# A transformer layer on one core: one modulation unit on TensorE and rounded activations first, with two value slots of the first heads inside the gate chunks

## The reference

```python
mod = silu(c) @ w_ada + b_ada                    # six vectors: sh1 sc1 gt1 sh2 sc2 gt2
h = rmsnorm(x, g_pre_mix) * (1 + sc1) + sh1
proj = h @ w_in                                  # gla q,k,v,r | rank-16 gate | moba q,k,v | gate_a, gate_b
y_a = (rmsnorm(gla_chunked(q, k, v, log_a)) * silu(gr)) @ w_gla_out      # 4 heads, dk 128, dv 256
y_b = moba_attention(mq, mk, mv) @ w_moba_out                            # 8 heads of 128, causal
y = (sigmoid(gate_a) * y_a + sigmoid(gate_b) * y_b) @ w_o
x = x + gt1 * rmsnorm(y, g_post_mix)
h = rmsnorm(x, g_pre_ffn) * (1 + sc2) + sh2
y = (gelu(conv3(h @ w_up)[g]) * conv3(h @ w_up)[u]) @ w_down
x = x + gt2 * rmsnorm(y, g_post_ffn)
```

## Time and profile before

| | |
|---|---|
| median of three runs | 1459.37 us (1457.54 to 1459.59) |
| profiled execution | 1459.07 us |
| its span | 1457.3 us |
| TensorE busy | 1422.6 us |
| VectorE busy | 1086.8 us |
| ScalarE busy | 760.2 us |
| DMA | 367.06 MB, mean 252 GB/s |
| granted TensorE clock | 0.999 |

### The profile page before, as it was taken

How to read it: one execution, slowest core, us unless ns; L and a number is a source line. 1 busy time by engine, 2 the same in 40 slices (tenths; PEclk the granted TensorE clock), 3 DMA queues, 4 the chain that set the end, 5 groups by cost and what they waited for, 6 DMA issues and landing times.

```text
span 1457.3 us, 19864 instructions
## 1 busy us (share of the span) xinstructions
PE 1422.6 (98%) x7296; PEld 1210.8 (83%) x7296; DVE 1086.8 (75%) x1161; ACT 760.2 (52%) x913; POOL 84.5 (6%) x165
## 2 busy tenths in 40 slices
PE   4999999999999999999999999999999999999998
PEld 3788788888888888878888888888888888888886
DVE  6899779898989878855787787777777766545545
ACT  5567763564545465443855545454555455443443
POOL 2000001111111100000000000000000000000000
PEclk9999999999999999999999999999999999999999
DMA  9999979998989777848477777677675555555653
GB/s 352 380 366 375 364 245 365 287 314 278 321 262 314 254 251 251 290 169 316 141 250 243 233 243 222 210 234 242 223 237 186 189 183 192 197 190 189 201 188 129
DMA packets 240569, 367.06 MB, mean 252 GB/s; under 512 B 12015, under 2 KB 178673, under 8 KB 239746
## 3 DMA queue, kind: packets, MB, share of 16 engines
q1 hardware_dynamic: 220576, 294.69, 60.9%
q0 software_dynamic: 18848, 69.23, 13.3%
q10 hardware_dynamic: 1090, 2.40, 0.4%
HBM read 364.18 MB, written 2.10 MB: 251 GB/s over the span
## 4 chain that ended last, share of the span: by engine, by line
PE 89%; ACT 3%; DMA 3%; DVE 3%; issue 1%; ACTq 0%; SPq 0%; DVEq 0%
PE ps L1465 88%; DMA raw<-in_w_in 2%; ACT hi L515 1%; DMA raw<-in_w_moba_out 1%; DMA rows<-in_b_conv 1%; ACT ps L556 0%; DVE lo L908 0%; DMA ada<-in_w_ada 0%; PE ps L1534 0%; DVE acc_a L937 0%; DVE yt L1285 0%; ACT h L561 0%; DVE x L1288 0%; ACT xn L543 0%; PE ps L1727 0%
## 5 line engine op out<-in xcount | busy, mean ns | idle before, releaser
L1465 PE MATMUL ps<-hT,hi 128*128 128x512 f32 x1936 | 466.2, 393 | 2.3 <-ACT ps L556 0.8
L1465 PEld LDWEIGHTS ps<-hT,hi 128*128 128x128 f32 x1936 | 355.8, 188 | 74.2 <-ACT ps L556 1.3
L515 ACT ACTIVATE hi<-raw 128x2048 fp32r<-128x2048 f32 (+1 forms) x123 | 222.3, 1808 | 241.5 <-DMA raw<-in_w_in 157.4
L908 DVE TENSOR_TENSOR lo<-raw,hi 128x2048 fp32r<-128x2048 f32 (+1 forms) x123 | 264.4, 2151 | 78.9 <-ACT hi L515 78.6
L1465 PEld LDWEIGHTS ps<-hT,lo 128*128 128x128 f32 x1920 | 246.1, 191 | 9.8 <-DVE lo L908 0.5
L1465 PE MATMUL ps<-hT,lo 128*128 128x256 f32 x1920 | 249.2, 283 | 0.1
L1413 DVE TENSOR_TENSOR lo<-raw,hi 128x2048 fp32r<-128x2048 f32 x88 | 199.0, 2290 | 33.3 <-ACT hi L851 32.9
L1465 PE MATMUL ps<-hi,hT 128*128 128x512 f32 x768 | 187.1, 394 | 3.2 <-DVE hT L962 2.1
L1465 PE MATMUL ps<-hi,asp 128*128 128x512 f32 x704 | 175.8, 389 | 0.0
L1465 PEld LDWEIGHTS ps<-hi,hT 128*128 128x128 f32 x768 | 141.9, 188 | 36.2 <-issue 4.4
L851 ACT ACTIVATE hi<-raw 128x2048 fp32r<-128x2048 f32 x88 | 165.7, 1906 | 9.4 <-DMA raw<-in_w_up 8.1
(11 more groups left out here) (262 smaller groups left out, 1317.3 us busy)
## 6 DMA issues: line engine op xcount, KB each, us to landing
raw<-in_w_up SPq DMA_DIRECT2D x176, 512.0 KB, 4.4
raw<-in_w_in SPq DMA_DIRECT2D x146, 512.0 KB, 6.0
ada<-in_w_ada POOLq DMA_DIRECT2D x128, 512.0 KB, 5.3
raw<-in_w_down SPq DMA_DIRECT2D x88, 512.0 KB, 4.1
adar<-in_w_ada SPq DMA_DIRECT2D x64, 384.0 KB, 8.2
raw<-in_w_o SPq DMA_DIRECT2D x32, 512.0 KB, 4.8
adar<-in_w_ada SPq DMA_DIRECT2D x16, 512.0 KB, 9.3
raw<-in_w_gla_out SPq DMA_DIRECT2D x16, 512.0 KB, 4.8
```

Source lines behind the costliest of these rows:

```text
L515: act.activation(hi[:, w % 4, 0:n], raw[:, w % 4, 0:n], ACT.Copy).then_inc(hi_done, 1)
L908: dve.tensor_tensor(lo[:, w % 4, 0:n], raw[:, w % 4, 0:n], hi[:, w % 4, 0:n].bitcast(F32), ALU.subtract).then_inc(lo_done, 1)
L1465: return pe.matmul(out_, lhsT, rhs, start=start, stop=stop, skip_group_check=open_sum)
```

## The change

Three things change together. **One unit on TensorE:** unit 12 of chunk 0 no longer goes through VectorE; six small products of its weights with the column `scol[:, 12]` open the sums in PSUM, and the sum of the other units is added to them. Three `spare` products go. The transposes of x start once its first 512 columns are scaled. **Rounded activations first:** for the first half of slot 0 VectorE writes the rounded h straight from x, TensorE multiplies it at once, and the products with the remainder of h come last. **Two value slots:** the first value slot (step 6) of heads 0 and 1 is moved to the middle of chunks 1 and 2, behind s = 3. ScalarE saves its sums in `vpart`, and copies them back to PSUM in step 5 of the head; step 6 has no slot any more, and decay products 0 to 3 move one step ahead in these heads. `vpart` takes the place of two `ada` buffers until the copies are done, so POOL uses three buffers instead of five up to unit 40.

```diff
+    GATE, VALUE, LOW = "gate", "value", "low"
+    EARLY = 2
...
+            if s_ == 3 and 1 <= q_ <= EARLY:
+                GATE_SLOTS.append((VALUE, q_, q_ - 1))
...
+    def head_steps(I):
+        return [n for n in range(HEAD_N) if n != 6 or I >= EARLY]
...
+    def gram_step(I, p):
+        return p + 3 if I >= EARLY or p > 3 else p + 2
...
+    PE_UNIT = 12
...
-    WIDE_FROM, WIDE_TO, THREE_TO = 8, 68, 86
+    THREE_FROM, WIDE_FROM, WIDE_TO, THREE_TO = 8, 40, 68, 86
...
+                if u == THREE_FROM:
+                    pool.wait_ge(tri_done, 1)
                 if u == WIDE_FROM:
-                    pool.wait_ge(tri_done, 1)
+                    pool.wait_ge(value_seed, EARLY)
...
-            for tt in range(TT):
-                act.activation(xn[:, tt, :], xn[:, tt, :], ACT.Copy, scale=stat[:, 2 + tt:3 + tt]).then_inc(xn_ready, 1)
+            for cs in (slice(0, 512), slice(512, D)):
+                for tt in range(TT):
+                    act.activation(xn[:, tt, cs], xn[:, tt, cs], ACT.Copy, scale=stat[:, 2 + tt:3 + tt]).then_inc(xn_ready, 1)
...
+                if kind == VALUE:
+                    act.wait_ge(used, w + 1)
+                    act.activation(vpart[:, s, :, :], ps[:, 6:8, :], ACT.Copy).then_inc(value_copy, 1)
...
-                    split_hi(w + 3)
+                    if streamed:
+                        split_hi(w + 3)
+                    if n == 5 and I < EARLY:
+                        b = 2 * group_pair(I, 3)
+                        act.wait_ge(evac, 5 * I + 3)
+                        act.activation(ps[:, b:b + 2, :], vpart[:, I, :, :], ACT.Copy).then_inc(value_seed, 1)
...
             for k in (0, 1):
-                ins = dve.tensor_scalar(h32[:, k, :], xT[:, k, TOK:], mods[:, M_SC1, k:k + 1], mods[:, M_SH1, k:k + 1], ALU.mult, ALU.add)
-            link(ins)
-            link(dve.tensor_copy(hT[:, 0:2, 0:TOK], h32[:, 0:2, :]))
-            dve.tensor_tensor(hT[:, 0:2, TOK:], h32[:, 0:2, :], hT[:, 0:2, 0:TOK].bitcast(F32), ALU.subtract).then_inc(h_ready, 1)
+                ins = dve.tensor_scalar(hT[:, k, 0:TOK], xT[:, k, TOK:], mods[:, M_SC1, k:k + 1], mods[:, M_SH1, k:k + 1], ALU.mult, ALU.add)
+            ins.then_inc(first_h, 1)
...
+                if b == 4:
+                    pe.wait_ge(cols_read, 2)
+                    pe.wait_ge(unit_in[PE_UNIT % 8], 32)
+                    for half in range(2):
+                        ins = unit_sums(half, unit_view(PE_UNIT), scol[:, PE_UNIT:PE_UNIT + 1], True)
+                    ins.then_inc(unit_used, 1)
...
-            for u in (KT - 3, KT - 2, KT - 1):
-                pe.wait_ge(unit_done, u)
-                spare(1)
...
+                if kind == VALUE:
+                    pe.wait_ge(sum_read, 2 * (K0[q + 1] - K0[1]))
+                    pe.wait_ge(hi_done, w + 1)
+                    tokens_still(w % 4, hT, 0, 6, True, True, w + 1).then_inc(used, 1)
+                    continue
...
+                    if n == 7 and I < EARLY:
+                        pe.wait_ge(value_seed, I + 1)
```

More of the change, by code:

```diff
@@ L64, in gate_at @@
     def gate_at(w):
-        q, s = divmod(w if w < W_LOW else w - 1, 8)
-        return q, s
+        return GATE_SLOTS[w][1:] if w < W_HEAD and GATE_SLOTS[w][0] == GATE else (None, None)
     def gate_stays(q, s):
@@ L349, in load_head @@
                 elif 6 <= n <= 9:
[L350 to L351 removed]
+                    load_values(w, I, 4 * (n - 6))
                 else:
@@ L570, in _ @@
             act.activation(hi[:, 0, 0:1024], raw[:, 0, 0:1024], ACT.Copy).then_inc(half_hi, 1)
-            act.wait_ge(arr[0], fills(0))
-            act.activation(hi[:, 0, 1024:slot_elements(0)], raw[:, 0, 1024:slot_elements(0)], ACT.Copy).then_inc(hi_done, 1)
+            act.wait_ge(first_ready, 1)
+            for k in range(2):
+                ins = act.activation(h32[:, k, :], xT[:, k, TOK:], ACT.Identity, bias=mods[:, M_SH1, k:k + 1], scale=mods[:, M_SC1, k:k + 1])
+            ins.then_inc(first_h32, 1)
             act.wait_ge(mods_ready, 1)
@@ L590, in gate_in_again @@
                 q, s = gate_at(w)
-                if w < W_LOW and gate_seeded(q, s):
+                if q is not None and gate_seeded(q, s):
                     act.wait_ge(gate_copy, through(gate_copied, q, s - 3))
@@ L1036, in gate_out @@
                 q, s = gate_at(w)
-                if w != W_LOW and gate_added(q, s):
+                if q is not None and gate_added(q, s):
                     dve.wait_ge(used, w + 1)
@@ L1040, in gate_out, with a_unit @@
                     dve.tensor_tensor(gate_sum(q, s), gate_sum(q, s), gate_banks(q, s), ALU.add).then_inc(gate_add, 1)
-            LAST_UNITS = [8 * q + 4 for q in range(NQ - 1)]
-            H_AT = [8 * q + 5 + (q == NQ - 2) for q in range(NQ - 1)]
+            def a_unit():
+                u = next(gate_units, None)
+                if u is not None:
+                    head_unit(u)
+            gate_units = iter(range(next_unit, NQ * KT))
             for w in range(W_HEAD):
-                q, s = gate_at(w)
+                kind, q, s = GATE_SLOTS[w]
                 if w > W_LOW:
                     gate_out(w)
-                if w == W_LOW:
+                if kind == LOW:
                     link(dve.memset(galow[0:32, :], 1.0))
@@ L1525, in _, with unit_sums @@
             pe.transpose(ps[:, 1, 0:nc_], rows[0:nc_, 5, :], ident[0:nc_, 0:nc_]).then_inc(colsT, 1)
-            pe.wait_ge(xn_ready, TT)
+            def unit_sums(half, values, vector, first):
+                js = range(2, CHUNK[0]) if half else range(2)
+                for j in js:
+                    for m in range(2):
+                        ins = mm(ps[:, half, 4 * m + j:4 * m + j + 1], values[:, m, P * j:P * (j + 1)], vector,
+                                 first and (j, m) == (js[0], 0), not first, True)
+                return ins
             for b in range(8):
-                if b == 6:
-                    pe.wait_ge(cols_read, 2)
+                if b in (0, 2):
+                    pe.wait_ge(xn_ready, TT * (b // 2 + 1))
+                if b >= 6:
+                    pe.wait_ge(xt_read, b - 5)
                 for j in range(2):
@@ L1697, in _ @@
                         ins.then_inc(gram_done, 1)
-                    if 3 <= n <= 10:
-                        gram(I, n - 3)
+                    if gram_at(I, n) is not None:
+                        gram(I, gram_at(I, n))
                     if n == 5:
```

195 lines of the change are left out of this document (117 added, 78 removed).

## The result

The changed kernel takes 1466.64 us (median of 7 runs, 1462.10 to 1469.74), the kernel before 1458.85 (7 runs, 1457.54 to 1459.59): ratio 1.0048, 95% interval 1.0037 to 1.0059. It is slower, by 7.8 us. The profiled execution is the fastest of the seven: 1462.10 us, span 1460.4, 3.1 over the span of before. The predicted sum was +2.6, the predicted time 1461.7 with a range up to 1467, at the upper end of which the median lies. So two things want explaining: the 3.1 us of the profiled execution, place by place, and the 4.5 us between it and the median, which no row of that execution shows.

What follows compares the result with a forecast made beforehand. TensorE, busy for 98% of the span, was taken as the bound, so time could only come from its waits. Terms 0 - 3.7 + 5.6 + 0.7 = +2.6 us on 1459.07 gave 1461.7, range 1456 to 1467.

Steps and rivals of the forecast that it cites:

- Term 1: Start up to slot 8: first product up to 3.8 us earlier, lead lost by slot 8; 0, bounds 0 and -3.
- edge of chunk 3: Edges of chunks 2 and 3: chain from the unit sums to h unaltered, 0.
- Term 2: Chunk 3 and low slot: value slots let DMA regain time, fewer waits; -3.7 us, bounds -4.6 and -2.5.
- Term 3: Heads 0 and 1: TensorE waits for value_seed, copied behind a conversion; +5.6 us, bounds 0 and +9.
- 4, head 0: Decay products one step earlier in head 0 wait for VectorE's first operands; +0.7 us, bounds 0 and +1.2.
- Term 4, head 1: Decay products one step earlier in head 1: covered by tail work, 0.
- two value slots in gates and not in heads: Twenty-four products per head leave the heads and are paid in the gates: 0.
- The allowance for a late fill: Heads 0 and 1: conversion ahead of the seed may wait for its fill; 0.2 us allowed each.
- the waits grow: Rival, heads 0 and 1: fill before the seed's conversion lands 1.5 us late in both; +3, 1464.7; chance 0.22.
- The clock: Rival: new long waits drop the array to 1.2 GHz; at most 2.7 us a time, +5.4 for two, 1467; chance 0.10.
- the three that were named: New TensorE waits expected: about 2.4 us before slot 8 and 2.6 us in each of heads 0 and 1.
- edge of 0.2%: Whole kernel: 0.2%, 2.9 us, separates a difference from no change; chances faster 0.23, same 0.40, slower 0.37.

Runs made afterwards that it cites:

- three moves: Changed kernel with the value_seed copy in step 4, head 1's oo in step 1, row sums of heads 0 and 1 all in step 6: 1456.69 us.
- 6: Changed kernel with the value_seed copy put ahead of the conversion in step 5: 1466.47 us, ratio 1.0049.
- 4: Changed kernel's start part alone, without value slots: 1458.73 us; its value slots alone, with the start of before: 1466.25 us.
- 7: Two kernels: three moves, 1456.69 us; the same with the value_seed copy in step 5, ahead of the conversion, 1459.74 us.
- 2: Changed kernel with ten unread products ahead of the value_seed wait in heads 0 and 1: 1465.08 us, ratio 1.0040.
- 3: Kernel before plus a ScalarE copy that TensorE awaits before step 6, heads 0 and 1: 1467.82 us; with ten unread products before the wait: 1465.48.
- 5: Changed kernel with head 1's oo ahead of the first selection: 1463.98 us; also copy in step 4: 1459.72; both, with the start of before: 1460.77.

## Why the prediction was right in its sum and too low for the median

The sum, term by term, for the profiled execution:

| term | predicted | measured | read from |
|---|---|---|---|
| 1, the start up to slot 8 | 0 | 0.0 | 69.48 against 69.46 |
| edge of chunk 3 | 0 | +0.6 | 40.11 - 34.06 - 5.41 |
| 2, chunk 3 and low slot | -3.7 | -3.6 | 38.48 against 42.09 |
| 3, the seeds | +5.6 | +5.3 | 3.39 + 3.54 - 2 x 0.80 (idle 2.35 + 2.50) |
| 4, head 0 | +0.7 | -0.4 | 270.22 - 187.53 against 262.74 - 179.66 |
| 4, head 1 | 0 | +2.0 | start of the first decay product, 2.47 behind the products before it against 0.44 (idle 1.86, for `oo`) |
| two value slots in gates and not in heads | 0 | -0.3 | 2 x (5.41 - 5.56) |
| behind the heads | - | -0.7 | the wait below is gone |
| sum | +2.6 | +2.9; by the spans +3.1 | 1460.4 and 1457.3 |

The 5.56 is a value slot in its head, from 271.26 to 276.82 in the kernel with three moves. At step 5 of head 2 the changed kernel is 3.71 us late (415.80 against 412.09). Some of that is made good at a place which the prediction did not look at, a wait of TensorE for `GA` behind the heads, in the trace of before:

```profile
565.72 1.09 PE L1727 MATMUL ps<-ident,GA 128*128 128x128 f32 x8 [0.49 <-DVE GA L1213]
```

The changed kernel does not wait there, and is 3.01 late behind it. That the sum came so near to the profiled execution is partly luck: the errors (+0.6, +2.0 and -0.3, -1.1, -0.3, -0.7) nearly cancel, and it was the one execution of seven in which the clock stayed at 0.999.

**Term 1** was right for its reason: the landing of slot 7 is set by bytes. Its size of lead was wrong in that execution, 1.2 and not up to 3.8 us, because I took the speed of the array at the start as given. VectorE did end its units earlier (27.94 against 28.69), but TensorE's queue was not through with what stands ahead of the sums. The transposes in rows (instructions, busy us, mean ns of one), before from 24 to 25 and from 26 to 27 us, and in the changed kernel from 27 to 28:

```profile
L1534 PE MATMUL ps<-ident,xn 128*128 128x128 f32 x7 | 1.7, 421 | 0.0
L1534 PE MATMUL ps<-ident,xn 128*128 128x128 f32 x7 | 0.9, 272 | 0.0
```

```profile
L1607 PE MATMUL ps<-ident,xn 128*128 128x128 f32 x7 | 1.7, 421 | 0.0
```

In the five traces with the start of before the array becomes fast between 23 and 27 us, among the transposes and ahead of the spare products (the first is at 26.64). With the new start it becomes fast near 25 us in one trace, between 29 and 31 in seven, and between 38 and 39 in the trace of 6. What differs ahead of these moments is that a wait of 0.96 us and the twelve one-column records of unit 12 now stand among the transposes; which of them matters, and whether the dropped spare products would have helped in the late case, no kernel tests. A lead is lost by slot 8; a lateness of 3 us is not, 2.05 of it arrives there. The slower group of runs in 4 and 7, whose clock column shows nothing, may be such late starts. That is argued from one trace; a late fill behind which the clock stays up would look the same, and no kernel tells the two apart.

**The edge of chunk 3** I had put at 0, "the chain from the unit sums to h is unaltered". It was unaltered, but a conversion that stands ahead of the row sums now waits for a fill that a value slot and its units have made later. In the traces it is 0.4 us of wait for h at that edge in the best and 2.1 in the worst.

**Term 2** came within 0.1, with the bounds 0.9 and 1.2 us away; the 6.5 us that its lateness starts from stand in no row of the prediction, so part of this closeness can be luck.

**Term 3** held in place, in mechanism and, by starts, in size. A wait of 0.56 is left where the conversion is taken out of the queue, nothing where the copy is a step earlier. The allowance for a late fill was 0.2 for each head; the fill was on time in the profiled execution, and 2.34 us late in the one of 2 (3.08 and 1.61 in the two of 3). That was the rival "the waits grow": it is true in some executions and not in others.

**Term 4, head 1**: "tail work covers it: 0" is the step that failed. The tail work is on TensorE; what I did not look up is that the first decay product of a later head also waits for `og_f`, because it writes the bank out of which VectorE makes `oo`. Moving that product a step earlier moved it in front of `oo`, which costs 2.0 us (1.9 of idle time). In head 0 the 0.7 was not needed: VectorE was ready, and the wait of 0.7 for `GA` at 228.09 of before had gone.

**The clock** was named with its mechanism and got a chance of 0.10; it is what happens in most executions. The reason for the low chance was that waits up to 1.24 us did nothing (the earlier trace rows even have one of 1.54), which said nothing on waits of 1.9 to 2.5, of which there were now three. They are not the three that were named: ahead of slot 8 there is no wait of 2.4 but the 1.24 of before, and the third is `oo`. The price was bounded at 2.7 us a time, it is 1.6 (5.5 against 3.9 us for sixteen products), but three places can have it, and the wait for h at the edge of chunk 3 as a fourth in 5: 3 x 1.6 = 4.8 us, and 1462.1 + 4.8 = 1466.9, where the median is 1466.64. So it is luck, too, that the range's upper end of 1467 (two falls of 2.7) lies just above the median (three of 1.6). The seven runs bear the price out: at a mean clock of 0.999 1462.1, at 0.998 and 0.997 1463.4 and 1463.8, at 0.996 1466.6, at 0.995 1466.9 to 1469.7. The two slowest, 1468.1 and 1469.7, lie above what three falls cost; late fills or the fourth place could add the rest, and no trace shows these runs. By the prediction's own edge of 0.2% the change is slower, to which it gave 0.37 against 0.40 for the same.

## What to carry to other kernels

A copy or a wait that TensorE needs goes into the step before, not behind the conversion of the same step: in an ordered queue each conversion may be waiting for a transfer, and everything behind it inherits that. When a stall is removed, look what is queued next: of the seeds, `oo` and the row sums (5.3, 2.0 and 2.0 us) the third showed only once the seeds were gone, and only with all three gone was the kernel faster than before. A wait of TensorE of about 2 us is to be priced at itself plus what the lower clock costs behind it, and one profiled execution may be the lucky one: set its clock beside that of the other runs before its sum is taken for the median.

## What was not expected of the hardware

- Waits of the same length have different effects: 2.35 us was followed by products at the full clock three times, 1.85 us once and 1.86 us twice at half of it (and 1.86 once at the full one). One fall costs 1.6 us.
- In the first 30 us the clock column reads 1.00 while twelve one-column products take 2.56 us (24.03) and twelve more 1.40 us (30.15) in the same trace; in the trace of 6 the second twelve take 2.56 as well. There the durations tell the array's rate and the column doesn't; two executions can so differ by 2 us at slot 8 that the column does not show.
- The fill ahead of step 5's conversion was on time in the profiled execution of the changed kernel and 2.34 us late in that of 2; on time in that of the kernel before, and 3.08 and 1.61 late in those of 3. In none of these had the order of the fills been changed.
